# State-space layer: weight splitting moved from GpSimd to ScalarE and VectorE, intra-chunk products ahead of inter-chunk products, loops over groups written out

## The reference

```python
def step(h, inp):                       # one chunk of Q rows, for 8 groups of 4 heads
    xc, dac, bc, cc = inp
    acum = jnp.cumsum(dac, axis=1)
    seg = acum[:, :, None] - acum[:, None, :]
    decay = jnp.exp(jnp.where(causal, seg, -jnp.inf))
    cb = jnp.einsum('btgn,bsgn->btsg', cc, bc)
    y_diag = jnp.einsum('btsg,btsgr,bsgrp->btgrp', cb, decay, xc)
    y_off = jnp.einsum('btgn,bgrpn,btgr->btgrp', cc, h, jnp.exp(acum))
    a_last = acum[:, -1]
    w_in = jnp.exp(a_last[:, None] - acum)
    h_new = h * jnp.exp(a_last)[..., None, None] + jnp.einsum('bsgn,bsgr,bsgrp->bgrpn', bc, w_in, xc)
    return h_new, y_diag + y_off

def ssd_mixer(x, ...):
    proj = x @ w_in                     # z, x/B/C and dt
    xbc, conv_new = causal_conv_silu(xbc, conv_prev, conv_w, conv_b)   # 4 taps, then silu
    y, hT = ssd_scan(xs, dt, A, Bm, Cm, h0)
    y = y + d_skip[:, None] * xs
    g = y * jax.nn.silu(z)              # then a root-mean-square norm in each group of 256 columns
    return normed @ w_out, conv_new, hT
```

## Time and profile before

| | us |
|---|---|
| median of 3 runs | 1716.01 (1713.54 to 1722.2) |
| the profiled execution, its own time | 1715.31 |
| its span | 1713.6 |
| TensorE busy in the span | 1686.4 (98%) |
| VectorE / GpSimd / ScalarE busy | 951.7 / 897.4 / 467.9 |
| the state-space groups 0 to 7, from the first `chunk_in` to the end of the last `mean_squares` | 56.93 to 461.2 |

### The profile page before, as it was taken

One profiled execution on the slowest core, in us unless ns is written; L12 is line 12 of the kernel. 1 busy time (PEld: TensorE's weight loads), 2 busy tenths in 40 slices (PEclk: granted clock), 3 DMA queues, 4 the chain that ended last, 5 costly groups with the idle time before them and its releaser, 6 DMA issues.

```text
span 1713.6 us, 31874 instructions
## 1 busy us (share of the span) xinstructions
PE 1686.4 (98%) x12252; PEld 1625.2 (95%) x12252; DVE 951.7 (56%) x1664; ACT 467.9 (27%) x816; POOL 897.4 (52%) x736
## 2 busy tenths in 40 slices
PE   8999999999999999999999999999999999999996
PEld 8899999999999999999999888999999999999996
DVE  6999999998846451222315733987255431313226
ACT  3344334444213340211202512111024420302105
POOL 4544444444455655555555265444556555555552
PEclk9999999999999999999999999999999999999998
DMA  5133322233222222222222322222222222222222
GB/s 189 69 105 101 99 94 98 68 99 99 70 77 85 74 85 86 75 85 86 79 81 77 127 85 81 66 68 77 81 80 82 79 86 84 77 86 86 75 86 68
DMA packets 45564, 148.03 MB, mean 86 GB/s; under 512 B 7200, under 2 KB 12704, under 8 KB 44320
## 3 DMA queue, kind: packets, MB, share of 16 engines
q1 hardware_dynamic: 37312, 130.50, 22.9%
q10 hardware_dynamic: 8160, 16.18, 2.9%
HBM read 141.50 MB, written 5.15 MB: 86 GB/s over the span
## 4 chain that ended last, share of the span: by engine, by line
PE 70%; DVE 2%; ACT 1%; issue 0%; ACTq 0%; DVEq 0%
PE ps L596 21%; PE ps L597 21%; PE ps L598 21%; PE ps L845 2%; PE ps L846 2%; PE ps L847 2%; PE ps L899 1%; DVE s L1630 0%; PE ps L900 0%; PE ps L855 0%; PE ps L856 0%; PE ps L901 0%; ACT r L1198 0%; DVE na L1795 0%; DVE vm L1942 0%
## 5 line engine op out<-in xcount | busy, mean ns | idle before, releaser
L596 PE MATMUL ps<-xh,wh 128*128 128x288 f32 (+1 forms) x1968 | 586.9, 298 | 8.1 <-DVE xl L1318 8.1
L518 POOL TENSOR_TENSOR wl<-wraw,wh 128x1024 fp32r<-128x1024 f32 x237 | 582.5, 2458 | 19.8
L598 PE MATMUL ps<-xh,wl 128*128 128x288 f32 (+1 forms) x1968 | 584.0, 297 | 0.0
L597 PE MATMUL ps<-xl,wh 128*128 128x288 f32 (+1 forms) x1968 | 583.9, 297 | 0.0
L596 PE MATMUL ps<-h,wh 128*128 128x288 f32 x1632 | 482.6, 296 | 0.0
L598 PE MATMUL ps<-h,wl 128*128 128x288 f32 x1632 | 480.9, 295 | 0.0
L597 PE MATMUL ps<-h,wh 128*128 128x288 f32 x1632 | 480.5, 294 | 0.0
L515 POOL TENSOR_TENSOR tick<-tick 128x1 f32<-128x1 f32 x237 | 56.0, 236 | 730.3 <-DMA wraw<-wstream 730.3
L596 PEld LDWEIGHTS ps<-xh,wh 128*128 128x128 f32 x1968 | 373.0, 190 | 8.4 <-DVE wl L1321 8.1
L598 PEld LDWEIGHTS ps<-xh,wl 128*128 128x128 f32 x1968 | 372.1, 189 | 0.0
L597 PEld LDWEIGHTS ps<-xl,wh 128*128 128x128 f32 x1968 | 371.8, 189 | 0.2
(11 more groups left out here) (243 smaller groups left out, 1705.2 us busy)
## 6 DMA issues: line engine op xcount, KB each, us to landing
wraw<-wstream SPq DMA_DIRECT2D x241, 512.0 KB, 3.4
acb<-acum_scratch ACTq DMA_DIRECT2D x8, 1152.0 KB, 6.8
out_y<-r SPq DMA_DIRECT2D x8, 288.0 KB, 2.3
xr<-x SPq DMA_DIRECT2D x3, 576.0 KB, 8.5
hs<-ssm_in ACTq DMA_DIRECT2D x8, 128.0 KB, 6.6
out_ssm_s<-hsn ACTq DMA_DIRECT2D x8, 128.0 KB, 5.9
out_ssm_p<-hp ACTq DMA_DIRECT2D x8, 128.0 KB, 1.9
bb<-bias_v ACTq DMA_DIRECT2D x1, 1024.0 KB, 4.9
```

The lines of the kernel that those rows point to most:

```text
L518: pool.tensor_tensor(m.wl[:, s], m.wraw[:, s], m.wh[:, s], ALU.subtract).then_inc(S.w_ready, 1)
L596: mm(out, w_hi, x[0], start=start, stop=False)
L597: mm(out, w_hi, x[1], start=False, stop=False)
L598: return mm(out, w_lo, x[0], start=False, stop=stop)
```

## The change

Until the sixth unit of the output projection GpSimd splits nothing (`U_POOL` = `U_WOUT` + 6). Units 2 to 54 are rounded by ScalarE (`weight_hi`) and subtracted by VectorE (`weight_lo`), each at a fixed place in that engine's list, six units in a group. In `chunk_out` the four intra products come first, then the two inter products. The loops over groups 1 to 6 on ScalarE and VectorE are written out.

```diff
+U_POOL = U_WOUT + 6
+def ssd_unit(g, j):
+    return U_SSD + 6 * (g + 1) + j
...
@@ pool_program
-    pool.wait_ge(S.w_ready, 2)
-    for u in range(2, 5):
+    pool.wait_ge(S.w_ready, U_POOL)
+    for u in range(U_POOL, U_POOL + 2):
         split_one(u)
-    run(5, (U_FFN0 - 5) // RING)
+    run(U_POOL + 2, (U_FFN0 - U_POOL - 2) // RING)
...
@@ tensor_program, chunk_out
-        for j in range(2):
-            for p in range(2):
-                e = 2 * j + p
-                last = mm(yb[p * HD:(p + 1) * HD, j * Q:j * Q + q], m.xdt[0:q, k, e * HD:(e + 1) * HD],
-                          m.dec[0:q, k, e, 0:q], start=True, stop=True)
-            if n > 0:
+        for e in range(HPG):
+            j, p = e // 2, e % 2
+            last = mm(yb[p * HD:(p + 1) * HD, j * Q:j * Q + q], m.xdt[0:q, k, e * HD:(e + 1) * HD],
+                      m.dec[0:q, k, e, 0:q], start=True, stop=True)
+        if n > 0:
+            for j in range(2):
                 last = mm(yb[:, (2 + j) * Q:(2 + j) * Q + q], h[:, j * P:(j + 1) * P], m.act[:, 1, t0:t0 + q],
                           start=True, stop=True)
...
@@ scalar_program
+    def weight_hi(u):
+        act.wait_ge(S.w_hi, u)
+        act.wait_ge(m.w_in[u % RING], 16 * (u // RING + 1))
+        f(m.wh[:, u % RING], m.wraw[:, u % RING], ACT.Copy).then_inc(S.w_hi, 1)
...
+    weight_hi(2)
+    weight_hi(3)
...
     raw_tile(0, 0, U_SSD)
+    weight_hi(4)
     raw_tile(0, 1, U_SSD + 1)
+    weight_hi(5)
...
     raw_tile(0, 2, U_SSD + 2)
+    weight_hi(6)
     raw_tile(0, 3, U_SSD + 3)
+    weight_hi(7)
...
@@ scalar_program, group
         exp_acum(g)
+        weight_hi(ssd_unit(g, 1))
+        weight_hi(ssd_unit(g, 2))
         for n in range(2, 5):
             if more:
                 raw_tile(g + 1, n - 2, 6 * g + (U_SSD + 4 + n))
             exp_decay(g, n)
             if n == 3 and not first:
                 round_y(g - 1)
+            weight_hi(ssd_unit(g, n + 1))
...
         f(m.y[:, :, :], m.gy[:, :, :], ACT.Square).then_inc(S.sq_ready, 1)
         if more:
+            weight_hi(ssd_unit(g + 1, 0))
             silu_conv(g + 1)
...
-    with act.Fori(1, GROUPS - 1) as g:
+    for g in range(1, GROUPS - 1):
         group(g, True)
...
@@ vector_program
+    def weight_lo(u):
+        s = u % RING
+        dve.wait_ge(S.w_ready, u)
+        dve.wait_ge(S.w_hi, u + 1)
+        tt(m.wl[:, s], m.wraw[:, s], m.wh[:, s], ALU.subtract).then_inc(S.w_ready, 1)
...
+    weight_lo(2)
+    weight_lo(3)
...
-    conv(0, 0)
-    conv(0, 1)
-    conv(0, 2)
+    for j in range(3):
+        conv(0, j)
+        weight_lo(4 + j)
...
     conv(0, 3)
+    weight_lo(7)
...
@@ vector_program, group
         before(g, 0)
         before(g, 1)
         if not first:
+            weight_lo(ssd_unit(g, 0))
             window(g)
...
         operands(g, 0)
         operands(g, 1)
+        weight_lo(ssd_unit(g, 1))
+        weight_lo(ssd_unit(g, 2))
         if more:
             conv_params(g + 1)
         after(g, 0)
...
         nxt(0)
+        weight_lo(ssd_unit(g, 3))
         before(g, 3)
...
         operands(g, 4)
+        weight_lo(ssd_unit(g, 4))
         if not first:
             split(g - 1)
+        weight_lo(ssd_unit(g, 5))
         nxt(2)
...
-    with dve.Fori(1, GROUPS - 1) as g:
+    for g in range(1, GROUPS - 1):
         group(g, True)
```

More of the change, by code:

```diff
@@ L1134, in layer_norm_deferred @@
         f(m.rstd[:, :, :], m.msq[:, :, :], ACT.Exp, scale=-0.5).then_inc(S.d_rstd, 1)
[L1136 to L1140, removed]
     def early_bias(k):
@@ L1251, in scalar_program @@
     early_bias(1)
-    v_weight_hi(U_V + 2)
+    weight_hi(U_V + 2)
     normed_tile(2)
-    v_weight_hi(U_V + 3)
+    weight_hi(U_V + 3)
     for k in range(3, 6):
@@ L1719, in early_gate_second @@
         tt(ta, ta, m.rstd[:, :, :], ALU.mult).then_inc(S.early_t, 1)
[L1721 to L1726, removed]
     def centred_tile(k):
@@ L1885, in vector_program @@
         if k == 4:
-            v_weight_lo(U_V + 2)
+            weight_lo(U_V + 2)
         elif k == 5:
@@ L1889, in vector_program @@
         elif k == 6:
-            v_weight_lo(U_V + 3)
+            weight_lo(U_V + 3)
     normed_lo(KT - 1)
```

## The result

The changed kernel takes **1724.65 us** (median of 11 runs, 1724.22 to 1725.92), the kernel before 1716.01 (11 runs, 1713.54 to 1722.2): a ratio of 1.0051 with an interval of 1.0041 to 1.006. That is 8.6 us slower, at the very edge of what I had called no change, 4.6 us above the predicted 1720 and inside the range. The profiled execution took 1724.22 us (span 1722.5, before 1713.6: +8.9).

A forecast was written before the change was run, and what follows sets the result against it. TensorE, 98% busy, bounded the kernel before; a ScalarE-VectorE ring would set groups 1 to 6. Start -1.4, group 0 -1.2, groups 1 to 6 +9.6, group 7 -1.9 make +5.1, rounded to +4.5: 1720 us, range 1706 to 1730.

The forecast's parts named there:

- The ring: Groups 1 to 6: ScalarE's roundings, VectorE's work to the gate, ScalarE to silu_conv close a 52.8 us loop; +9.6 us.
- VectorE's idleness: VectorE ahead of a group's second weight_lo: idle 4 to 6 us until ScalarE's rounding releases it.
- the wait at chunk_out(3): TensorE in each of groups 1 to 6 waits about 1.6 us there for m_ready, the decay product.
- What VectorE gets back: From after(0) to the gate's end, decay products, additions and gate lose GpSimd's hold-ups: 5.5 us a group.
- Rival C: VectorE doesn't get its 5.5 us back; ring up to 58.3 us a group, time up to 1753; chance 0.18.
- The products: Intra before inter products in chunk_out save 0.35 us per 128-row chunk, 0.2 in the 64-row one, 1.2 a group.
- rival B: The products' new order brings nothing; groups 0 and 7 lose 2.4 us, 1722.5 us; chance 0.06.
- Group 7: Last group, without conv: VectorE gets ahead, the wait at the last mean_squares goes; -1.9 us.
- The start: Ahead of group 0: without GpSimd beside the conv, the 1.4 us wait at the first chunk_in goes; -1.4 us.
- The sum: Whole kernel: start, group 0, groups 1 to 6 and group 7 add up to +5.1 us, rounded down to +4.5.

The follow-up runs named there:

- e1: Changed kernel with ScalarE's roundings of a group's second and third unit moved ahead of rms and exp_acum: 1707.37 us.
- e7: Changed kernel with ScalarE's rounding for the next group's first unit moved behind silu_conv: 1725.1 us.
- e2: Changed kernel with the old order of chunk_out's products (intra, intra, inter, twice): 1726.45 us.
- e9: Changed kernel with the roundings ahead of rms, GpSimd's first split behind the last sum_squares, and the old order of products: 1712.39 us.
- e5: Changed kernel with GpSimd's first split waiting until VectorE's sum_squares of the last group is done: 1718.85 us.
- e6: Changed kernel with VectorE's subtractions for the second and third unit moved behind after(0) and before(2): 1720.55 us.
- e8: Changed kernel with both edits, ScalarE's second and third rounding ahead of rms and GpSimd's first split behind the last sum_squares: 1701.81 us.
- e3: Kernel before with only the new order of chunk_out's products, inter behind all four intra: median 1715.52 us, runs 1705.67 to 1722.65.

## Why the prediction was right, and where it was wrong

**The ring: right.** "52.8 us a group" came out as 52.57, from 11.0 + 35.7 + 5.9 against the predicted 11.2 + 35.7 + 5.9. For six groups that makes +8.3 instead of +9.6. VectorE's idleness (5.16 us) and the wait at chunk_out(3) (1.4 us, predicted 1.6) are where they should be. At chunk_in the row of waits has 0.3 us (predicted 0.5 to 0.7), and for the second unit 0.2 (predicted 0.6); these rows count less than TensorE loses, for the pitch is 2.7 us above e1's 49.84 and they add up to 1.9. Where the other 0.8 us lie isn't shown. e1 and e7 show that it is the ring, since the one shortens it and the other only turns it.

**What VectorE gets back: right.** The rows of VectorE's products and the gate, grouped by line over the whole changed kernel (columns: instruction and count, then busy us and mean ns, then idle time before it):

```profile
L1338 DVE TENSOR_TENSOR wl<-wraw,wh 128x1024 fp32r<-128x1024 f32 x55 | 67.1, 1219 | 38.6 <-ACT wh L948 38.3
L1501 DVE TENSOR_TENSOR dec<-dec,cbm 128x512 f32<-128x512 f32 (+1 forms) x40 | 25.1, 627 | 0.9 <-ACT dec L1031 0.9
L1548 DVE TENSOR_TENSOR gy<-y,zs 128x1152 f32<-128x1152 f32 x8 | 12.7, 1581 | 0.0
```

Full decay products take 0.68 us. The gate takes 1.35 us in seven groups and 3.21 in the eighth, where GpSimd subtracts beside it. So the shortest row of before, 2.02, was no gate by itself: 1.34, from the row of the same size, was the price. The rule of the Trainium skill ("SBUF — State Buffer", Who interferes with whom), by which the two instructions exclude each other for a whole instruction, agrees: the subtraction of 460.80 ends at 463.26, and the gate, begun at 461.26, ends 1.21 us behind that, at 464.47, about its own length. Rival C needed gates above 2 us and falls with this row.

**The products: right in size, 0.34 us a chunk for 0.35.** The 64-row chunk gave 0.29 where I took 0.2. Among the six products of a chunk there were three switches between the two kinds and now there is one, not two and one as I had written ahead of the prediction: two switches less for 0.34 us, 0.17 each. That they are worth nothing in the ring holds too (e2: 1.8 us over the whole kernel); rival B falls with e9, where the old order costs 1.33 us a group.

**Group 7: wrong, and this is the step that failed.** The prediction put it: "Group 7 has no conv, so VectorE gets ahead: -1.2 for the products, -1.3 for the wait at L776, +0.6 for its second unit: -1.9." It measured +2.6, and +1.8 more behind it, of which the lower clock explains 1.1 to 1.6. VectorE did get ahead, but I had priced this stretch as if GpSimd stayed still to its end. The diff says otherwise: `pool.wait_ge(S.w_ready, U_POOL)` lets GpSimd go as soon as the subtraction of unit 54 is done, at 455.3, and that lies ahead of VectorE's last chunk and last gate. With it came 2.19 us for the hdec product, 1.86 for the gate and 0.43 for the residual: 4.5 us, on the path to the last mean_squares. The same rule that I had used for the benefit would have given the cost. e5 takes 5.8 us back by that one line: its group 7 is at 44.65 us, 2.3 less than before, where I had said 1.9 less, and its 1718.85 us lie 1.2 under the forecast.

**The start: right; the microsecond on top is luck.** The wait at the first chunk_in went (-1.4). Besides, TensorE's products stand 0.24 us apart at first and 0.13 later in both kernels; the change of pace came at 12.67 us before and at 10.85 now, so some 7.6 products more at 0.11 less, 0.8 us. The view gives a granted clock of 1.00 there throughout, but the trace's record of the clock only begins at those two moments, and 0.24 is also the distance of these products in e6 at 0.50 (170.57 to 173.45). So until then TensorE ran at the lower level. The moment is not the change's doing: in the eight traces of kernels that share this start (the changed one, e1, e2 and e5 to e9) it lies between 10.85 and 14.14, and the first chunk_in between 54.55 and 56.01, in the same order of kernels. The changed kernel's profiled execution has the earliest of all. In e8 the moment is 12.92, about that of the kernel before, and the first chunk_in starts at 55.44, 1.5 us earlier than before, for the 1.4 predicted. What sets the moment isn't shown.

**The sum.** -2.4 - 1.4 + 8.3 + 2.6 + 1.8 = +8.9. The terms that I had worked out gave +5.1, rounded down to +4.5. The rounding down was no help: the ring's own misses (1.3 us) and the start's (1.0) did point that way, but group 7 outweighed them. The forecast held because the largest term, the ring, was right; the start's microsecond belongs to the one profiled execution, the fastest of the eleven.

## What to carry to other kernels

Before handing one engine's work to two others, write down the ring that their lists form, with what each piece takes alone: it can set the pitch with neither engine over 53% busy, and the cure is to place the added work where the engine that receives it would wait anyway (e1: two calls moved, 17 us). Where an engine is kept silent for the sake of another, look at the moment when it is let go again, and at what its first work meets there (e5: one wait, 5.8 us). A local gain on the bounding engine shows only where that engine is the bound: the same order of products was worth 10.6 us in one kernel and 1.8 in another.

## What the runs showed of the hardware

A stall of TensorE can cost more than its length: the granted clock falls to 0.50 (1.2 GHz) during it or right behind it, and stays there while TensorE is at work again. How long it was low, and the wait beside it: 6.8 us in the changed kernel (wait of 3.89) and in e7 (3.91), 6.8 us twice in e3 (3.32 and 3.26), but 3.4 us in e1 (3.87), e2 (3.54) and e6 (3.87). In these the fall comes while TensorE still waits. Beside the waits of 1.3 and 1.4 us of the kernel before, and the six of 1.4 in the changed one, the clock stayed at 1.00; yet in e6 it also fell for 3.4 us behind a stall of 0.85. So the length of the wait alone doesn't decide, and what else does stays open.

With it the spread of a kernel's runs can be read. The changed kernel, in which GpSimd is silent through groups 0 to 6, spreads over 1.7 us in 11 runs and e8 over 0.9 in 4; the kernel before spreads over 8.7 in 11, and e3 over 17 in 10. In e3's trace each group that is over 7 us longer is one episode of a GpSimd subtraction beside VectorE, a wait of TensorE, and a lowered clock. That the spread of the kernel before has the same cause is likely, but none of its slower executions was traced.
